# Seven block products in place of eight for a third of the feed-forward entry tiles of a two-layer encoder step, on one core

## The chip, the core and the metric

One core of a Trainium2 chip runs the whole program. The metric is the time of one execution on the device in microseconds (us), the median of several runs. The engines work side by side and meet only at semaphores: PE (TensorE, matmuls), DVE (VectorE), ACT (ScalarE), POOL (GpSimd) and SP (SyncE, which here issues most transfers). PEld is the weight load of a matmul.

## The reference, cut to what matters

Two request groups, 512 prompt tokens and 64 sample tokens, go through two layers with shared weights. Each layer is a feed-forward block (half step), a mixer (two kinds of attention, a spatial gate, and a merge of the three branches under gates) and a second feed-forward block. Shift, scale and gate of every normalization come from a vector c per group through a large matrix `w_ada`. In float32:

```
mp = silu(c) @ w_ada[l] + b_ada[l]                 # 9 modulation vectors of 1024 per layer
pre_mod(h, g, shift, scale) = rmsnorm(h, g) * (1 + scale) + shift
g, u = split(x @ w1)                               # x: 576 x 1024, w1: 1024 x 5504
swiglu(x) = (silu(g) * u) @ w2                     # 2752 -> 1024
h += 1/2 * gate * rmsnorm(swiglu(pre_mod(h)))      # feed-forward block, twice a layer
m = sig(gA)*(oA@W_a) + sig(gB)*(oB@W_b) + sig(gC)*(oC@W_c);  h += gate2 * rmsnorm(m @ W_out)
```

## The kernel before

Activations lie transposed: 128 features on the partitions, 576 tokens along them, in two halves of 288 (`columns(b)`). Every float32 product is three matmuls of rounded parts: weights and activations are each split in a high part (fp32r) and a low rest, and `w_hi*x_hi + w_hi*x_lo + w_lo*x_hi` is summed in PSUM. So one 128x128 weight block against 576 tokens is 6 matmuls (3 products, 2 halves), and one tile of 128 output features of the feed-forward entry (1024 inputs, 8 blocks) is 48.

**Weights** come in chunks of 128x1024 float32 (8 blocks, 512 KB) through a ring of 5 slots (`SLOTS`). SP issues the transfer for chunk c when PE is done with chunk c-5. ACT then writes `w_hi` (`split_hi`, L1296), DVE writes `w_lo = w_raw - w_hi` (`split_lo`, L1715; it lies where the raw chunk lies), and PE may start. The order of these steps among the other work of ACT and DVE is written out by hand.

**Feed-forward entry** (`f1a`, `f1b`, function `ffn_up`): 22 pairs i of a g tile and a u tile (43 chunks; pair 21 is a half-filled tail). In each pair PE makes g into PSUM pair 0 (banks 0 and 1) and u into PSUM pair 1 (banks 2 and 3). DVE takes each out of PSUM times `r2`, the reciprocal root mean square per token (`take`, L1792), since x is normalized only behind the product; the share of the shift comes from two more columns of the matmul (290 in place of 288). ACT does silu, DVE the product g*u, and both split it in `hid_hi` and `hid_lo`. PE may use a PSUM pair again when it has been taken (`acc_free`).

**Feed-forward exit** (`f2a`, `f2b`): 8 output tiles of 126 matmuls and a tail. **Gate stage** (`merge`, phase `gate`): for each of 8 tiles m, PE makes three gate tiles of 48 matmuls (br 0, 1, 2 into PSUM pairs 0, 1, 0) and then three branch products A, B, C of 12, 24 and 12 matmuls into pairs 1, 0, 1. A needs the release of gate tile br 1, B that of br 2 (the `sig` instruction, L2343, and the small one behind it), C that of A (`msum`, L2350).

**Modulation units**: what `w_ada` needs is cut in units of 128 outputs x 512 inputs, 256 in all. POOL issues the 256 KB transfer of a unit into one of two buffers (`ada_w`) when DVE has finished the unit two before it. DVE then does two multiply-and-sum instructions per unit (L1729), one for each group. Tables in the kernel (`ADA_STAGES`, `f1_units`, `f2_units`, `gate_units`) say how many units stand at each place of DVE's order: up to 3 in a pair of an entry, 2 at a step of the exits of layer 0, and 1 or 2 ahead of `sig` of br 1 and br 2 in the gate stage of layer 0. POOL otherwise only issues transfers.

Of the kernel before, what the change touches and what calls it, by code (L numbers as in the profile page):

```python
# [70 lines left out]
F1_CHUNKS = 2 * KF - 1  # L71
# [15 lines left out]
ADA_STAGES = [((0, "f1a"), (2, 4, 3)), ((0, "f2a"), (5, 7)), ((0, "gate"), (6,)), ((0, "f1b"), (8, 10, 9)),  # L87
              ((0, "f2b"), (11, 13)), ((1, "f1a"), (12, 14, 15)), ((1, "f2a"), (16,)), ((1, "gate"), ()),
              ((1, "f1b"), (17,)), ((1, "f2b"), ())]
AFTER_PAIRS = ((0, "gate"), (1, "f1b"))  # L90
# [33 lines left out]
def f1_units(l, ab, i):  # L124

    return 0 if i in (2, 11, KF - 2) else 1 if (l, ab) == (1, "b") else 3


def f2_units(l, ab):

    half = {(0, "a"): 8, (0, "b"): 8, (1, "a"): 4, (1, "b"): 0}[l, ab]
    return iter([2] * half + [0] + [2] * half + [0] * KF)


def gate_units(m):

    return {1: (1, 1), 2: (1, 2), 3: (1, 2), 4: (0, 0), 5: (1, 1), 6: (1, 2), 7: (1, 2)}.get(m, (0, 0))
# [16 lines left out]
def chunk(l, ph, i):  # L154
    return l * CHUNK_N + CHUNK_AT[ph][0] + i

# [215 lines left out]
def build_program(nc, ins, outs):  # L372
# [64 lines left out]

    rms = sb("rms", [P, 3, TOK], at=big + 2 * TOK * 4)
# [122 lines left out]
    hid_ready = S("hid_ready", 2 * KF)  # L561
# [29 lines left out]
    sil_ready = S("sil_ready", 2 * KF)  # L591
    g_scaled = S("g_scaled", 4)
# [79 lines left out]
    def _(sp):  # L672
# [38 lines left out]

        def exchange_tail(l, f):
# [6 lines left out]
        for l in range(DEPTH):  # L719
            for i in range(F1_CHUNKS):  # L720
                load(l, "f1a", i, ins["f1"], 2 * l * F1_CHUNKS + i)
                if l == 0 and i == 1:
                    first_ada(*FIRST_PARTS[1])
                if l == 0 and i == 2:
                    first_ada(*FIRST_PARTS[2])
                    first_ada(*FIRST_PARTS[3])
            for name, out in (("cache_a_k", "roll_k"), ("cache_a_v", "roll_v")):
# [15 lines left out]
            for i in range(F1_CHUNKS):  # L743
                load(l, "f1b", i, ins["f1"], (2 * l + 1) * F1_CHUNKS + i)
# [12 lines left out]
    def _(pe):  # L757
# [32 lines left out]
        def whole_chunk(l, ph, i, p, group, hi, lo, cols, gate=None):  # L790
# [8 lines left out]
            r.then_inc(chunk_done.sem, 1)  # L799

# [117 lines left out]
        def ffn(l, ab, n):  # L918
# [361 lines left out]
    def _(act):  # L1280
# [4 lines left out]
        def split_hi():  # L1285
# [5 lines left out]
            act.wait_ge(raw_full[c % SLOTS].sem, raw_full[c % SLOTS].done(0, c // SLOTS))  # L1291
# [5 lines left out]

        def chunk_over(l, ph, i):
            act.wait_ge(chunk_done.sem, chunk_done.done(0, chunk(l, ph, i)))

        def ffn_up(l, ab):
            ph, at = "f1" + ab, (0 if ab == "a" else KF + KD)
            mine = 0 if ab == "a" else KF
# [10 lines left out]
            for i in range(KF - 1):  # L1314
                if i == 1 and not l and ab == "a":
                    split_hi()
                if i < 2:
                    act.wait_ge(g_scaled.sem, g_scaled.done(l, (ab == "b") * 2 + i))
                else:
                    split_hi()  # L1320
                    act.wait_ge(acc_free[0].sem, acc_free[0].done(l, GROUP_AT[ph][0] + i - 1))
# [6 lines left out]
                if i > 1:  # L1328
                    split_hi()
            split_hi()  # L1330
# [3 lines left out]
            act.wait_ge(hid_ready.sem, hid_ready.done(l, mine + KF - 1))  # L1334
            copy(hid_hi[:, KF - 1, :], tail_hid[:, :]).then_inc(prod_hi.sem, 1)

# [379 lines left out]

# [963 lines left out]
```

## Time and profile before

| | us |
|---|---|
| median of 3 runs | 2680.75 (2680.7 to 2681.24) |
| the profiled execution | 2681.71 |
| its span, first to last instruction | 2679.8 |
| PE busy | 2645.8 (99%) |
| DVE busy | 1636.2 (61%) |
| ACT busy | 963.1 (36%) |
| POOL busy | 200.0 (7%), all but four tiny instructions the issue of transfers |

The page lists the busy time of each engine, then the chain of work that ended last, then groups of instructions with their mean duration. PE is busy all the time, and its clock was granted in full. So what matters is how many matmuls there are, and whether anything makes PE wait.

### The profile page before, as it was taken

Reading aid. Unit: us, or ns where it says so; the run is one execution under the profiler, and the core shown is the slowest. Engines: PE = TensorE matmul, PEld = TensorE weight load, DVE = VectorE, ACT = ScalarE, POOL = GpSimd, SP = SyncE. Lnnn points to the kernel's source line nnn. Section 1 sums busy time; section 2 is a strip of 40 time slices with the busy share of each in tenths; the row PEclk is TensorE's granted clock in tenths of the full one; section 3 lists DMA queues with packets and bytes.
Section 4 is the critical chain, followed back from the end, with each engine's and each line's share of the span. In section 5 each row is a group of like instructions: output and inputs, shape, how many; then the busy total and the mean of one; then the engine's idle time right before and its main releaser. Section 6 shows DMA issues by size and latency. Waiting matters only on the chain.

```text
span 2679.8 us, 49072 instructions
## 1 busy us (share of the span) xinstructions
PE 2645.8 (99%) x20698; PEld 2563.3 (96%) x20698; DVE 1636.2 (61%) x3542; ACT 963.1 (36%) x1792; POOL 200.0 (7%) x371
## 2 busy tenths in 40 slices
PE   7999999999999999999999999999999999999997
PEld 6999999888999999999999999998889999999997
DVE  4677666765555577776577776276655445555523
ACT  4232324444422442232252223255452336322321
POOL 0111010110000001111101111001100000000000
PEclk9999999999999999999999999999999999999998
DMA  6444453343333224445424444234332222333321
GB/s 261 126 146 141 157 177 113 124 130 109 95 111 111 87 95 154 136 144 168 131 89 152 139 159 161 88 98 141 119 105 80 87 83 76 99 109 105 95 82 65
DMA packets 92987, 324.79 MB, mean 121 GB/s; under 512 B 13980, under 2 KB 17628, under 8 KB 92064
## 3 DMA queue, kind: packets, MB, share of 16 engines
q1 hardware_dynamic: 62512, 221.72, 26.3%
q0 software_dynamic: 30256, 99.93, 11.2%
q8 instruction: 164, 2.69, 0.4%
q14 instruction: 55, 0.45, 0.1%
HBM read 310.70 MB, written 11.55 MB: 120 GB/s over the span
## 4 chain that ended last, share of the span: by engine, by line
PE 97%; DVE 1%; DMA 0%; issue 0%; ACT 0%; DVEq 0%; SPq 0%; ACTq 0%
PE ps L769 90%; PE ps L1131 2%; PE ps L1179 1%; PE ps L1155 1%; PE ps L778 1%; DMA ada_first<-in_ada_first 0%; PE ps L1148 0%; PE ps L823 0%; DVE prob L2242 0%; PE ps L909 0%; PE ps L1192 0%; DVE next L1792 0%; PE ps L807 0%; PE ps L832 0%; PE ps L1055 0%
## 5 line engine op out<-in xcount | busy, mean ns | idle before, releaser
L769 PE MATMUL ps<-x_hi,w_hi 128*128 128x288 f32 (+1 forms) x4224 | 938.9, 298 | 2.4 <-DVE x_lo L1883 1.5
L769 PE MATMUL ps<-x_lo,w_hi 128*128 128x288 f32 (+1 forms) x4224 | 922.5, 294 | 0.0
L769 PE MATMUL ps<-x_hi,w_lo 128*128 128x288 f32 (+1 forms) x4224 | 922.4, 294 | 0.0
L769 PEld LDWEIGHTS ps<-x_hi,w_hi 128*128 128x128 f32 x4224 | 682.6, 188 | 14.2 <-issue 8.0
L769 PEld LDWEIGHTS ps<-x_hi,w_lo 128*128 128x128 f32 x4224 | 685.7, 188 | 0.0
L769 PEld LDWEIGHTS ps<-x_lo,w_hi 128*128 128x128 f32 x4224 | 685.3, 188 | 0.3
L1715 DVE TENSOR_TENSOR w_lo<-w_raw,w_hi 128x1024 fp32r<-128x1024 f32 x384 | 468.1, 1222 | 160.1 <-ACT w_hi L1296 158.1
L1296 ACT CAST w_hi<-w_raw 128x1024 fp32r<-128x1024 f32 x384 | 391.9, 1048 | 72.4 <-DMA w_raw<-in_f 71.6
L769 PE MATMUL ps<-hid_hi,w_hi 128*128 128x288 f32 x1344 | 301.1, 295 | 0.0
L769 PE MATMUL ps<-hid_lo,w_hi 128*128 128x288 f32 x1344 | 299.3, 293 | 0.0
L769 PE MATMUL ps<-hid_hi,w_lo 128*128 128x288 f32 x1344 | 299.0, 294 | 0.0
L1729 DVE CUSTOM_DVE_ANT_0 ps<-ada_w,c_half,ada_all 128x512 f32<-128x512 f32 x256 | 193.6, 756 | 108.8 <-DMA ada_w<-in_ada 108.6
L2432 POOL DMA_DIRECT2D ada_w<-in_ada x256 | 138.1, 540 | 1626.6 <-DVE ada_all L1729 1622.1
L769 PEld LDWEIGHTS ps<-hid_hi,w_hi 128*128 128x128 f32 x1344 | 219.8, 188 | 0.2
L769 PEld LDWEIGHTS ps<-hid_lo,w_hi 128*128 128x128 f32 x1344 | 219.4, 188 | 0.2
L769 PEld LDWEIGHTS ps<-hid_hi,w_lo 128*128 128x128 f32 x1344 | 217.2, 187 | 0.0
L1327 ACT CAST hid_hi<-hid 128x576 fp32r<-128x576 f32 x84 | 56.6, 674 | 446.7 <-DVE hid L1765 446.7
L1729 DVE CUSTOM_DVE_ANT_0 ada_w<-ada_w,c_half,ada_all 128x512 f32<-128x512 f32 x256 | 191.5, 748 | 0.0
L1323 ACT ACTIVATE sil<-sil,z 128x512 f32<-128x512 f32 (+1 forms) x168 | 80.9, 529 | 248.6 <-DVE z L1793 248.4
L1792 DVE TENSOR_TENSOR hid<-ps,r 128x576 f32<-128x576 f32 x80 | 60.6, 758 | 146.9 <-PE ps L769 146.9
L1808 DVE TENSOR_TENSOR acc_y<-acc_y,sq 128x576 f32<-128x576 f32 (+1 forms) x51 | 33.0, 646 | 179.5 <-ACT sq L1367 153.7
L1367 ACT ACTIVATE sq<-ps 128x576 f32<-128x576 f32 x38 | 24.9, 654 | 296.1 <-PE ps L778 263.2
(243 smaller groups left out, 2440.4 us busy)
## 6 DMA issues: line engine op xcount, KB each, us to landing
w_raw<-in_f SPq DMA_DIRECT2D x260, 512.0 KB, 3.7
ada_w<-in_ada POOLq DMA_DIRECT2D x256, 256.0 KB, 4.0
w_raw<-in_gate SPq DMA_DIRECT2D x64, 512.0 KB, 3.6
w_raw<-in_tri SPq DMA_DIRECT2D x40, 512.0 KB, 3.7
ada_first<-in_ada_first SPq DMA_DIRECT2D x4, 2048.0 KB, 21.0
w_raw<-in_wout SPq DMA_DIRECT2D x16, 512.0 KB, 3.6
c_half<-c_scratch POOLq DMA_DIRECT2D x11, 512.0 KB, 5.6
decay_p<-f_prompt POOLq DMA_DIRECT2D x8, 512.0 KB, 4.5
```

Source lines behind the costliest of these rows:

```text
L769: r = mm(ps[:, 2 * out + b, 0:width], w, xx[:, cols(b)], start=first and n == 0, stop=last and n == 2)
L778: r = mm(ps[:, 2 * out + b, 0:HALF], w[:, s, t * P:(t + 1) * P], hid_hi[:, k, columns(b)], start=False, stop=w is w_lo)
L1131: r = mm(out, q_st[rows, i * P:i * P + m], k, start=True, stop=True)
L1155: r = turn_in(out, prob[0:m, place(u), b * P:b * P + w], const[0:m, IDENT, 0:m])
L1296: copy(w_hi[:, c % SLOTS, :], w_in[:, c % SLOTS, :]).then_inc(hi_ready.sem, 1)
L1323: r = A(sil[:, i, part], sil[:, i, part], ACT.Silu, bias=c_col[:, 2 * (i % 2), g:g + 1])
L1327: copy(hid_hi[:, i, :], hid[:, i, :]).then_inc(prod_hi.sem, 1)
L1715: V.tensor_tensor(w_lo[:, s, :], w_in[:, s, :], w_hi[:, s, :], ALU.subtract).then_inc(lo_ready.sem, 1)
L1729: r = V.tensor_tensor_reduce(out, ada_w[:, u % 2, :], c_half[:, g, :], 1.0, so_far, ALU.mult, ALU.add, so_far)
L1792: V.tensor_tensor(two(dst), pair[p], two(r2[:, :]), ALU.mult)
L1808: V.tensor_tensor(total, total, more, ALU.add).then_inc(y_added.sem, 1)
L2432: nc.gpsimd.dma_start(dst, src).then_inc(signal.sem, 16)
```

## The change

**Seven products.** In pairs 6 to 12 (`JOIN0` to `JOIN1`) of each of the four entries, g and u tile of a pair are made together. The inputs are cut in two halves of 512 features, the tokens in two halves of 288, the weights in four block columns (g or u, lower or upper inputs): a 2x2 by 2x2 block product, done with 7 half products of 12 matmuls (4 blocks, 3 parts, 288 tokens) in place of 8. It needs sums of weight blocks (4 additions of 128x512 a pair, done by POOL in place in the raw slots, `sum_of_w`), sums of blocks of x (`t_sums`, once an entry), and 7 additions of a 128x288 product out of PSUM (`join_parts`, DVE). A pair is now four chunks (three of 1024 columns, one of 512) whose high and low parts ACT and DVE make behind the sums.

**x normalized ahead.** The block sums need plain x. So DVE multiplies h by `r2` (`h_times_r2`), ACT adds scale and shift (`full_of_h`), both split the result again while pair 3 runs (`high_of_full`, `low_of_full`; pair 3 and pair 4 go through the inputs g and u in step), and from pair 4 on g and u need no `r2` and no shift columns: ACT reads g from PSUM in its silu, DVE multiplies u out of PSUM.

**Modulation units moved.** Pairs 3 to 12 have none any more. The tables put 5, 5, 6, 0, 4, 4, 4, 4 of them in pairs 13 to 20 (three of the four entries), 32 in place of 16 in the exit `f2a` of layer 1, 32 in place of 16 in the gate stage of layer 0 and 16 in place of 0 in that of layer 1. There are 256 as before. In the diff, `load_joined` is in the program of SP, `joined_pair` in that of PE, `joined_stage` in that of DVE and `sum_of_w` in that of POOL.

```diff
-def f1_units(l, ab, i):
-    return 0 if i in (2, 11, KF - 2) else 1 if (l, ab) == (1, "b") else 3
+def f1_units(l, ab, i):
+    if (l, ab) == (1, "b"):
+        return 2 if i >= JOIN1 else 0
+    return {13: 5, 14: 5, 15: 6, 17: 4, 18: 4, 19: 4, 20: 4}.get(i, 0)
...
-    half = {(0, "a"): 8, (0, "b"): 8, (1, "a"): 4, (1, "b"): 0}[l, ab]
+    half = {(0, "a"): 8, (0, "b"): 8, (1, "a"): 8, (1, "b"): 0}[l, ab]
...
-def gate_units(m):
-    return {1: (1, 1), 2: (1, 2), 3: (1, 2), 4: (0, 0), 5: (1, 1), 6: (1, 2), 7: (1, 2)}.get(m, (0, 0))
+def gate_units(l, m):
+    if l == 0:
+        return {1: (2, 3), 2: (2, 3), 3: (3, 3), 5: (2, 3), 6: (2, 3), 7: (3, 3)}.get(m, (0, 0))
+    return {1: (1, 1), 2: (1, 2), 3: (1, 2), 5: (1, 1), 6: (1, 2), 7: (1, 2)}.get(m, (0, 0))
...
+        def load_joined(l, ab, i):
...
+                sp.wait_ge(chunk_done.sem, chunk_done.done(0, c + v - SLOTS))
+                spare_read(l, ab, c + v)
...
+        def joined_pair(l, ab, i):
...
+            part(0, 0, 0, *x_block(0, 0)).then_inc(half_done.sem, 1)
+            part(1, 0, 1, *t_block(2)).then_inc(chunk_done.sem, 1)
+            part(2, 1, 0, *t_block(1)).then_inc(half_done.sem, 1)
+            part(3, 1, 1, *t_block(3)).then_inc(chunk_done.sem, 1)
+            part(4, 2, 0, *t_block(0)).then_inc(half_done.sem, 1)
+            part(5, 2, 1, *x_block(half_k, 0)).then_inc(chunk_done.sem, 1)
+            part(6, 3, 0, *x_block(half_k, 1)).then_inc(chunk_done.sem, 1)
...
+        def joined_stage(l, ab, i):
+            more = i + 1 < JOIN1
+            if i > JOIN0:
+                low_of_joined(l, ab, i, 2)
+                low_of_hid(l, ab, i - 1)
+            join_parts(l, ab, i, 0)
+            join_parts(l, ab, i, 1)
+            if i > JOIN0:
+                low_of_joined(l, ab, i, 3)
+            join_parts(l, ab, i, 2)
+            join_parts(l, ab, i, 3)
+            join_parts(l, ab, i, 4)
+            if more:
+                low_of_joined(l, ab, i + 1, 0)
...
+            join_parts(l, ab, i, 5)
+            join_parts(l, ab, i, 6)
+            if more:
+                low_of_joined(l, ab, i + 1, 1)
...
+            product_of_joined(l, ab, i)
...
+        def sum_of_w(l, ab, i, order):
...
+            if order == 0:
+                pool.wait_ge(raw_full[g].sem, raw_landed(c))
...
+            elif order == 1:
+                pool.wait_ge(w_sum.sem, w_sum.done(l, at))
+                pool.wait_ge(raw_full[u].sem, raw_landed(c + 1))
...
+            elif order == 2:
+                pool.wait_ge(w_sum.sem, w_sum.done(l, at + 1))
+                pool.wait_ge(chunk_done.sem, chunk_done.done(0, c + 3 - SLOTS))
...
+            else:
+                pool.wait_ge(raw_full[more].sem, raw_landed(c + 2))
...
+            nc.gpsimd.tensor_tensor(*operands, ALU.add).then_inc(w_sum.sem, 1)
```

The order of DVE in the gate stage of layer 0, tile m=1, from the low part of a weight chunk through the units to `sig` of br 2, before (an ISA row over ps or ada_w is one of a unit's two instructions, the short rows read its sum):

```order
L1715 TENSOR_TENSOR w_lo<-w_raw,w_hi 128x1024 [waits hi_ready]
L1729 ISA ps,ada_all<-ada_w,c_half,ada_all 128x512 [waits ada_full1]
L1729 ISA ada_all 128x1
L1729 ISA ada_w,ada_all<-ada_w,c_half,ada_all 128x512
L1729 ISA ada_all 128x1
L2343 TENSOR_TENSOR sig<-ps,r_71 128x576 [waits chunk_done]
L2344 TENSOR_SCALAR z<-ps,b_gate 128x2
```

And DVE in the same place of the changed kernel, from the second of the three units that now stand behind the low part:

```order
L2112 ISA ps,ada_all<-ada_w,c_half,ada_all 128x512 [waits ada_full1]
L2112 ISA ada_all 128x1
L2112 ISA ada_w,ada_all<-ada_w,c_half,ada_all 128x512
L2112 ISA ada_all 128x1
L2112 ISA ps,ada_all<-ada_w,c_half,ada_all 128x512 [waits ada_full0]
L2112 ISA ada_all 128x1
L2112 ISA ada_w,ada_all<-ada_w,c_half,ada_all 128x512
L2112 ISA ada_all 128x1
L2772 TENSOR_TENSOR sig<-ps,r_71 128x576 [waits chunk_done]
L2773 TENSOR_SCALAR z<-ps,b_gate 128x2
```

Ahead of `sig` of br 2, which releases PSUM pair 0 for branch product B, stand three units where one stood here (two at m=2 and 3), on two buffers.

The order of DVE from the middle of one joined pair into the next in the changed kernel, where `ps` rows of 128x288 take products out of PSUM:

```order
L2057 TENSOR_TENSOR sil<-sil,ps 128x288 [waits half_done]
L2057 TENSOR_TENSOR hid<-hid,ps 128x288 [waits joined]
L2002 TENSOR_TENSOR w_lo<-w_raw,w_hi 128x1024 [waits hi_ready,w_sum]
L2057 TENSOR_TENSOR sil<-sil,ps 128x288 [waits chunk_done]
L2057 TENSOR_TENSOR sil<-sil,ps 128x288 [waits joined,chunk_done]
L2002 TENSOR_TENSOR w_lo<-w_raw,w_hi 128x1024 [waits hi_ready,w_sum]
L2064 SCALAR_TENSOR_TENSOR hid<-hid,sil 128x576 [waits joined,sil_half]
L2002 TENSOR_TENSOR w_lo<-w_raw,w_hi 128x1024 [waits hi_ready,w_sum]
L2070 TENSOR_TENSOR hid_lo<-hid,hid_hi 128x576 [waits prod_hi]
```

Before, a pair's low parts followed two PSUM reads of 128x576; now the low part that the next pair starts with stands behind the fifth of seven reads of 128x288, and it also waits for POOL's sums (`w_sum`).

## Rows read from the trace of the kernel before

**Rows 1.** The page: busy us (share of the span) and instructions of each engine.

```profile
PE 2645.8 (99%) x20698; PEld 2563.3 (96%) x20698; DVE 1636.2 (61%) x3542; ACT 963.1 (36%) x1792; POOL 200.0 (7%) x371
```

**Rows 2.** The chain that ended last: start us, us, what ran.

```profile
355.21 16.58 PE ps L769 x126
...
423.66 8.29 PE ps L769 x63
...
689.01 233.08 PE ps L769 x1767
...
955.26 267.83 PE ps L769 x2034
...
2005.73 233.51 PE ps L769 x1767
...
2557.89 16.59 PE ps L769 x126
```

**Rows 3.** Stages: us, busy us (instructions) by engine, clock, DMA share, GB/s.

```profile
690.00:922.00 232.00, 232.00 (x1763) 232.00 (x1762) 129.00 (x210) 75.66 (x122) 9.34 (x17) 1.00 0.33 102
...
955.00:1223.00 268.00, 268.00 (x2037) 267.95 (x2036) 193.35 (x400) 81.40 (x113) 27.67 (x51) 1.00 0.42 136
```

**Rows 4.** DVE by form: xcount, busy us, mean ns, idle before and its releaser.

```profile
L1715 DVE TENSOR_TENSOR w_lo<-w_raw,w_hi 128x1024 fp32r<-128x1024 f32 x384 | 468.1, 1222 | 160.1 <-ACT w_hi L1296 158.1
L1729 DVE CUSTOM_DVE_ANT_0 ps<-ada_w,c_half,ada_all 128x512 f32<-128x512 f32 x256 | 193.6, 756 | 108.8 <-DMA ada_w<-in_ada 108.6
...
L1770 DVE TENSOR_TENSOR hid_lo<-hid,hid_hi 128x576 fp32r<-128x576 f32 x84 | 63.8, 759 | 62.2 <-ACT hid_hi L1327 62.2
...
L1792 DVE TENSOR_TENSOR hid<-ps,r 128x576 f32<-128x576 f32 x80 | 60.6, 758 | 146.9 <-PE ps L769 146.9
...
L1849 DVE SCALAR_TENSOR_TENSOR rms<-ps,rms 128x288 f32<-128x288 f32 x12 | 5.5, 455 | 0.2
```

**Rows 5.** DVE in time, gate stage, m=5: start us, us, instruction [idle before].

```profile
765.17 0.76 DVE L2343 TENSOR_TENSOR sig<-ps,r 128x576 f32<-128x576 f32 x1 [0.90 <-PE ps L769]
765.84 0.21 DVE L2344 TENSOR_SCALAR z<-ps,b_gate 128x2 f32<-128x2 f32 x1
768.02 1.23 DVE L1715 TENSOR_TENSOR w_lo<-w_raw,w_hi 128x1024 fp32r<-128x1024 f32 x1 [1.97 <-ACT w_hi L1296]
769.16 0.75 DVE L1729 CUSTOM_DVE_ANT_0 ps<-ada_w,c_half,ada_all 128x512 f32<-128x512 f32 x1
...
771.86 0.75 DVE L2343 TENSOR_TENSOR sig<-ps,r 128x576 f32<-128x576 f32 x1
772.52 0.21 DVE L2344 TENSOR_SCALAR z<-ps,b_gate 128x2 f32<-128x2 f32 x1
773.18 0.76 DVE L2350 TENSOR_TENSOR msum<-sig,ps 128x576 f32<-128x576 f32 x1 [0.45 <-PE ps L769]
```

**Rows 6.** DVE in time, exit of layer 0, two groups of two units.

```profile
345.74 0.76 DVE L1729 CUSTOM_DVE_ANT_0 ps<-ada_w,c_half,ada_all 128x512 f32<-128x512 f32 x1 [1.19 <-DMA ada_w<-in_ada]
...
347.09 0.76 DVE L1729 CUSTOM_DVE_ANT_0 ps<-ada_w,c_half,ada_all 128x512 f32<-128x512 f32 x1
...
352.18 0.76 DVE L1729 CUSTOM_DVE_ANT_0 ps<-ada_w,c_half,ada_all 128x512 f32<-128x512 f32 x1 [2.52 <-DMA ada_w<-in_ada]
```

**Rows 7.** POOL in time, the same stretch: issues of the units' transfers.

```profile
341.41 0.54 POOL L2432 DMA_DIRECT2D ada_w<-in_ada  x1 [4.28 <-DVE ada_all L1729]
...
347.47 0.54 POOL L2432 DMA_DIRECT2D ada_w<-in_ada  x1 [3.89 <-DVE ada_all L1729]
```

**Rows 8.** The page: transfers, KB each, median us from issue to landing.

```profile
w_raw<-in_f SPq DMA_DIRECT2D x260, 512.0 KB, 3.7
ada_w<-in_ada POOLq DMA_DIRECT2D x256, 256.0 KB, 4.0
```

**Rows 9.** DVE in time, a pair of an entry: two instructions beside POOL's issues.

```profile
179.30 1.22 DVE L1715 TENSOR_TENSOR w_lo<-w_raw,w_hi 128x1024 fp32r<-128x1024 f32 x1
...
187.37 1.23 DVE L1715 TENSOR_TENSOR w_lo<-w_raw,w_hi 128x1024 fp32r<-128x1024 f32 x1 [0.19 <-ACT w_hi L1296]
```

**Rows 10.** POOL in time, the same pair.

```profile
179.65 1.09 POOL L2432 DMA_DIRECT2D ada_w<-in_ada  x2
```

More of the change, by code:

```diff
@@ L799, in whole_chunk, with chunk_pair @@
             r.then_inc(chunk_done.sem, 1)
+        def chunk_pair(l, ph, i, pairs, cols, ab):
+            c = chunk(l, ph, 2 * i)
+            chunk_ready(c)
+            chunk_ready(c + 1)
+            for k in range(KD):
+                n = (ab == "b") * KD + k
+                if i == NORMED:
+                    pe.wait_ge(x_full_ready.sem, x_full_ready.done(l, n))
+                for s in (0, 1):
+                    r = split_tile(pairs[s], c + s, k, x_hi[:, k, :], x_lo[:, k, :], cols, k == 0, k == KD - 1)
+                    if k == KD - 1:
+                        r.then_inc(chunk_done.sem, 1)
+                if i < NORMED and k < KD - 1:
+                    r.then_inc(x_read.sem, 1)
@@ L1313, in ffn_up @@
                 split_hi()
-            for i in range(KF - 1):
+            for i in range(NORMED):
                 if i == 1 and not l and ab == "a":
@@ L1327, in ffn_up @@
                 copy(hid_hi[:, i, :], hid[:, i, :]).then_inc(prod_hi.sem, 1)
-                if i > 1:
+                if i == 1:
                     split_hi()
+                    for k in range(KD):
+                        full_of_h(l, ab, k)
+                        if k == 3:
+                            split_hi()
+            for i in range(NORMED, KF - 1):
+                if JOIN0 <= i < JOIN1:
+                    joined_parts(l, ab, i)
+                    continue
+                if i == JOIN1:
+                    high_of_hid(l, ab, i - 1)
+                if i == JOIN0 - 1:
+                    high_of_joined(l, ab, JOIN0, 0)
+                    high_of_joined(l, ab, JOIN0, 1)
+                else:
+                    split_hi()
+                if i == NORMED:
+                    for order, t in enumerate((2, 1, 3, 0)):
+                        high_of_t(l, ab, t, order)
+                act.wait_ge(chunk_done.sem, chunk_done.done(0, chunk(l, ph, f1_chunk(i))))
+                A(two(sil[:, i, :]), pair[0], ACT.Silu).then_inc(acc_free[0].sem, 1)
+                if i == JOIN0 - 1:
+                    high_of_joined(l, ab, JOIN0, 2)
+                    high_of_joined(l, ab, JOIN0, 3)
+                    continue
+                if i > NORMED:
+                    split_hi()
+                act.wait_ge(acc_free[1].sem, acc_free[1].done(l, GROUP_AT[ph][1] + f1_group(1, i)))
+                copy(hid_hi[:, i, :], hid[:, i, :]).then_inc(prod_hi.sem, 1)
             split_hi()
@@ L1768, in ffn_up @@
                 r.then_inc(hid_ready.sem, 1)
+                if i == 1:
+                    for k in range(2, KD, 2):
+                        h_times_r2(k)
                 dve.wait_ge(prod_hi.sem, prod_hi.done(l, at + i))
```

394 lines of the change are left out of this document (350 added, 44 removed).

## The prediction, made before the changed kernel ran

> **What bounds the kernel now.** I read three views, in this order. The page's busy times: PE 99%, DVE 61%, POOL 7% [rows 1]. The chain that ended last: it is PE nearly throughout, in pieces of hundreds of matmuls without a break; an entry is 2034 matmuls in 267.83 us, so one matmul costs 0.1317 us. A run of 63 in which each follows the last into the same PSUM bank takes 8.29 us, 0.1316 each [rows 2]. So the pace does not hang on alternating banks, which half products of 12 don't do, nor on 290 or 288 columns, so that dropping the shift columns is worth nothing. The stages: in an entry DVE is busy 193 of 268 us, in the gate stage of layer 0 129 of 232, and that stage's chain (233.08) is no longer than layer 1's (233.51), which has no modulation units [rows 2, 3]. So nothing but the number of matmuls sets the end, and a change gains 0.1317 us for each matmul it drops as long as DVE, ACT, POOL and the transfers stay out of PE's way.
>
> **Part 1, seven products.** 84 matmuls a pair in place of 96: 12 x 0.1317 = 1.58 us. 7 pairs x 4 entries = 28 pairs: **-44.2 us**, if PE runs through. A pair is then 84 x 0.1317 = 11.06 us.
>
> DVE in such a pair: three low parts of 1024 columns (1.22) and one of 512 (0.69, on the line through the rows of 576 and 1024), seven additions out of PSUM (0.455), the product and the low part of `hid` (0.76 each) [rows 4]. 3.66 + 0.69 + 3.19 + 1.52 = 9.06 of 11.06 us. It fits, with 2 us to spare. The place without slack is the low part that the next pair starts with. It stands behind the additions of product 4; product 4 ends two products (24 matmuls, 3.16 us) before the pair does; 0.2 until DVE sees it, two additions 0.91, the low part 1.22: 0.8 us are left. That makes PE wait for nothing, by these rows.
>
> POOL's sums: the trace has no addition on POOL. The chain through them is: sum 2 may start behind product 5 (1.58 us before the pair ends), then sum 3, then a low part of 1.22 that is needed 24 matmuls (3.16 us) into the next pair. 1.58 + 3.16 - 1.22 - 0.2 = 3.3 us for two sums, so up to 1.65 us each they cost nothing. Lower bound 0.69 (DVE's own pace): 0. Upper bound 2.44, twice DVE's row for 1024 columns: 2 x (2.44 - 1.65) = 1.6 us a pair, all of the gain. The nearest rows are the 0.69 to 1.22 of DVE [rows 4], so I take 0.
> The Trainium skill (GPSIMD Engine Reference, section 3) has an addition of 2048 float32 columns at 4497 ns on GpSimd against 2293 ns on VectorE; by that pace a sum of 512 is, as an estimate of mine, about 1.2 us, and the term stays at 0.
>
> **Part 2, x ahead.** In pairs 2 to 5 DVE gets 3 x 1.36 (`h_times_r2`, 1152 columns on the line through the rows of 576 and 1024), 8 x 0.76 (low parts of x), 8 x 1.36 (block sums of x and their low parts), and loses all units and half of the PSUM takes: some 42 us of the 50.6 that four pairs last. What a pair needs stands half a pair or more ahead. I take 0; the bounds are 0 (no matmul is dropped here, so nothing can be gained) and 2 us an entry, one late low part.
>
> **Part 3, the units.** This is what I think decides. In the gate stage [rows 5] `sig` of br 2 starts at 771.86, at once behind the second of two units that began at 769.16, so a unit takes 1.35 us. The release of PSUM pair 0 is at about 772.7; PE has then nearly finished branch A (its `msum` starts at 773.18) and goes on to B into that pair. So the slack is 0.3 us, and the two units just fit. Now three stand there, and there are two buffers. In an exit one sees how fast a buffer comes back [rows 6, 7]: the unit that began at 345.74 ended at 347.09, POOL issued at 347.47, and DVE, waiting for it, began at 352.18: 5.09 us from a unit's end to the next in the same buffer. (The page's 4.0 [rows 8] is the median of all landings; here another transfer was under way, as it will be.) So:
> - (2, 3), at m=1, 2, 5, 6. Two units ahead of br 1 delay its `sig` by 0.4 (765.17 to 765.6) and the following low part to 768.4. Units 3 and 4 run to 770.9 and 772.25. Unit 5 needs unit 3's buffer: 770.9 + 5.09 = 776.0, ends 777.35. `sig` and its small follower take 0.9: 778.2. B could have begun at 773.0: **5.2 us** of waiting PE, four times, 20.8.
> - (3, 3), at m=3, 7. The third unit ahead of br 1 waits for its buffer to 769.3, so `sig` of br 1 comes at 770.65, just in time for A. The next low part ends at 774.6, units at 775.95, 777.3, and the last at 781.05 + 1.35 = 782.4; release 783.3: **10.3 us**, twice, 20.6.
> Gate stage of layer 0: **+41.4 us**. The pattern of layer 1 is the one that layer 0 had before [rows 5]: 0. Exit `f2a` of layer 1 gets layer 0's pattern, which holds up nothing: its tiles of 126 matmuls take 16.58 us each, as in the last exit, which has no units [rows 2]: 0.
>
> Entries, pairs 13 to 20. Two buffers give one unit per (1.35 + 5.09) / 2 = 3.2 us. Count from the end of u of pair 13, with the units in groups of 2 | 3, 2 | 3, 3 | 3 around the products, and about 1.2 and 0.7 for low parts between: the third unit of a group waits 3.7. Product 14 is done at 17.6 (PE needs it at 19.0), the next eight units put product 15 at 37.0, and PE needs it at 5 x 6.32 = 31.6: **5.4 us**. Pair 16 has no unit and DVE catches up; 4 units a pair (12.9 of 12.64 us) hold to the end. Three entries have this table: **+16.2 us**. If the buffer came back in 4.0 + 0.4 us, both terms would be 36 and 9.
>
> **Part 4, POOL and DVE side by side.** Does a POOL instruction that reads and writes SBUF hold up DVE? A low part beside two of POOL's issues takes 1.22 us, without any 1.23 [rows 9, 10], but an issue is no addition. Bounds: 0, and a full exclusion of each sum from the low parts. Then sum 1 puts 1.0 us ahead of the third low part, the additions move on, DVE comes to the critical low part after sum 2 has begun (product 5 is done by then) and waits 1.2 more: 1.0 + 1.2 - 0.8, minus 0.2 that the additions of products 0 and 1 had spare, is 1.2 us a pair, 34 us in all. I take 0.3 us a pair, since only one of four sums falls on the place without slack and the rows lean to none: **+8.4 us**.
> The Trainium skill (SBUF — State Buffer, section "Who interferes with whom") says that a DVE instruction with two SBUF inputs and a GpSimd instruction that reads SBUF exclude each other for their whole length. No row here shows it; by that rule the sum would take the upper end, and it is rival B.
>
> **Sum.** -44.2 + 41.4 + 16.2 + 8.4 = +21.8 us. The profiled execution is 2681.71 (span 2679.8), 0.96 over the median, so span 2701.6, that execution 2703.5, median 2680.75 + 21.8 = **2702.5**.
>
> **Rivals.**
> A, the forecast: the units' buffers make PE wait, the joined pairs run nearly free. 2702; with 36 and 9 for the terms of part 3 and 0 for part 4 it is 2681.5, with 12 more in part 4 2715. Chance 0.42.
> B, exclusion in full: joined pairs of 12.3 us give 10 us back instead of 44. 2680.75 + 57.6 - 10.2 = 2728. For: DVE has only 0.8 us at the critical place. Against: no row. Chance 0.25. It decides from 0.8 us of delay of that low part.
> C, faster: the buffers are no limit. If every transfer were there in time, three units cost 4.05 where 2.7 fitted: `sig` of br 2 released at 774.5, PE waits 1.5 us six times, 9 us, and none in the entries. 2680.75 - 44.2 + 9 = 2646. For: the median landing of 4.0 [rows 8] is shorter than the 4.7 I used. Against: DVE waits for its units at both groups of the exit, 1.19 and 2.52 us [rows 6], although only two stand in each. Chance 0.2.
> D, the seven products don't pay at all: sums over 1.65 us or late low parts stretch a pair to 12.64. 2680.75 + 57.6 = 2738 or more. Chance 0.08. The rest, 0.05, is what I haven't seen.
>
> **How the numbers follow.** The likeliest is A: 2702. For 8 in 10, the range takes most of A, B and the slow half of C: **2658 to 2734**. A measurement of this kernel tells 0.2% (5.4 us) from no change. Faster by more: most of C, 0.2. Within: between C and A, with short landings, 0.12. Slower: 0.68.
>
> **What would show it.** In the profile after: PE matmuls 20698 - 336 = 20362. The chain of a joined pair 11.06 us (A) or some 12.3 (B). In the gate stage of layer 0 a wait of PE for the `sig` instruction of br 2, six times, 5 to 10 us, the stage near 274 us and layer 1's still 233. In three entries one wait of PE in pair 16 for the product, about 5 us. DVE's wait for `ada_w` well over the 108.8 us of before [rows 4]. POOL additions near 1 us. If the gate stage stays at 233, part 3 is wrong and the kernel is faster; if DVE's low parts are longer than 1.22 in pairs 6 to 12, part 4 is.

## The result and the profile after

| | before | after |
|---|---|---|
| median of the runs, us | 2680.72 (2680.33 to 2681.24) | 2727.7 (2725.95 to 2729.09) |
| ratio to before | | 1.0175, interval 1.0157 to 1.0192 |
| profiled execution; its span, us | 2681.71; 2679.8 | 2725.95; 2724.0 |
| granted clock, mean over the span | 0.997 | 0.985 |

The changed kernel is 47 us slower; 2702 was forecast, 21.8 slower. The sign is right and the time lies in the range, but the loss is more than twice the forecast. The first page lines of after, which answer to [rows 1] and [rows 8] (busy us, share of the span, instructions; the clock in 40 slices; transfers with KB each and median us to landing):

```profile
PE 2630.2 (97%) x20362; PEld 2543.7 (93%) x20362; DVE 1731.3 (64%) x3522; ACT 1069.6 (39%) x1920; POOL 362.4 (13%) x484
...
PEclk9999999999989999999999999999999999999998
...
ada_w<-in_ada POOLq DMA_DIRECT2D x256, 256.0 KB, 3.4
```

PE has the 20362 matmuls that were forecast, 336 fewer, and yet is busy only 15.6 us less, in a span 44.2 us longer. So there are two losses: 60 us more in which PE stands, and some 29 us in which what it does takes longer (the 336 dropped matmuls were 44.2 us of work, and its busy time fell by only 15.6).

The chain that ended last says where (start us, us, what ran). The joined pairs of the first entry, the gate stage of layer 0 with the piece behind it, and the gate stage of layer 1; [rows 2] has the gate stages before:

```profile
114.82 77.98 PE ps L934 x588
...
724.29 13.39 PE ps L875 x84
756.82 14.17 PE ps L875 x84
792.19 38.82 PE ps L875 x276
849.66 13.83 PE ps L875 x84
882.70 12.74 PE ps L875 x84
916.67 49.53 PE ps L875 x363
966.69 9.87 PE ps L875 x75
...
2048.60 233.15 PE ps L875 x1767
```

588 matmuls of seven joined pairs take 77.98 us, 11.14 a pair: PE runs through. The gate stage of layer 0, one piece of 1767 matmuls before, has come apart: six pieces of it show here, each behind a wait, and between them the chain runs through DVE; layer 1's is one piece still. By the starts of the same piece in both chains the account is (us, after less before; what has gathered since the start of the program):

| at the start of | before | after | gathered | this stage |
|---|---|---|---|---|
| exit, layer 0, first | 320.98 | 317.79 | -3.2 | entry -3.2 |
| behind the gate stage, layer 0 | 922.57 | 966.69 | +44.1 | gate stage +47.3 |
| exit, layer 0, second | 1223.62 | 1266.97 | +43.3 | entry -0.8 |
| exit, layer 1, first | 1637.54 | 1680.29 | +42.7 | entry -0.6 |
| behind the gate stage, layer 1 | 2239.73 | 2282.24 | +42.5 | -0.2 |
| exit, layer 1, second | 2540.78 | 2582.88 | +42.1 | entry -0.4 |

Behind the last matmul some 2 us more follow (2.5 in the kernel with the tables alone, below, which has eight products; what makes them stays open). So the gate stage loses 47.3 us, and the entries, each with 84 matmuls less (-11.05 us), give 0.4 to 3.2. PE's waits of after (line that waits, releaser: us in total, times, longest):

```profile
PE ps L875 <- DVE z L2773: 33.4, 6, 7.0
PE ps L875 <- ACT sil L1579: 13.6, 4, 4.7
...
PE ps L875 <- DVE w_lo L1992: 11.0, 5, 3.2
...
PE ps L875 <- DVE hid L2187: 0.6, 2, 0.4
```

L2773 is the small instruction behind `sig` of br 2. (A wait of 11.1 at the program's start, left out, was there before.) L1579 is the silu of the plain g tiles, L1992 a low part outside the joined pairs: both belong to the entries, and neither is in the forecast. L2187 is the product of g and u, for which 5.4 us in pair 16 of three entries were forecast.

**The gate stage.** The chain there at m=2, from the end of the first unit behind the low part to PE's start at 756.82 (start us, us, what); it answers to [rows 5]:

```profile
749.19 0.61 DVE ada_w L2112
...
750.10 4.41 DMA ada_w<-in_ada
...
755.97 0.67 DVE sig L2772
756.64 0.14 DVE z L2773
```

The unit ends at 749.8, POOL issues, and the transfer lands at 754.5: 4.7 us from a unit's end to the next in its buffer. Then the third unit, `sig`, and PE may go on. PE waited 4.92 us. It then needed 14.17 us for 84 matmuls that take 11.06 at full pace. The stage in stretches around the wait at m=1 (stretch, us, then busy us and count of PE, PEld, DVE, ACT, POOL, granted clock, DMA share, GB/s):

```profile
709.00:719.00 10.00, 10.00 (x78) 10.00 (x77) 7.13 (x19) 1.90 (x3) 1.61 (x3) 1.00 0.41 113
...
724.30:729.00 4.70, 4.70 (x20) 4.70 (x21) 1.82 (x2) 1.86 (x3) 0.00 (x0) 0.52 0.17 56
729.00:738.00 9.00, 9.00 (x70) 9.00 (x69) 5.31 (x7) 1.63 (x2) 0.00 (x0) 1.00 0.23 61
```

Behind the wait the granted clock is 0.52, the lower level of 1.2 GHz for nearly all of 4.7 us, and PE is busy throughout with 20 matmuls where 36 would fit. Then it is 2.4 GHz again. The pieces behind the six waits take 54.1 us for four times 84 matmuls, 38.8 for 276 and 49.5 for 363; at 0.1317 each they would take 44.2, 36.3 and 47.8: 14.1 us lost to the clock. 33.4 + 14.1 = 47.5, the 47.3 of the table.

**The entries.** PE's timeline, the waits in the second entry (start us, us, instruction [idle before, releaser]), the chain that leads to each (as above), and the stretches behind them:

```profile
1019.95 0.82 PE L875 MATMUL ps<-x_hi,w_hi 128*128 128x288 f32 x2 [3.17 <-DVE w_lo L1992]
```

```profile
1013.47 3.81 DVE x_full L2210 x3
...
1018.67 1.14 DVE w_lo L1992
...
1019.95 15.53 PE ps L875 x96
...
1046.60 1.37 DVE t_raw L2015
1047.99 2.21 ACT t_hi L1493 x2
1050.20 0.56 ACT sil L1579
...
1050.89 12.88 PE ps L875 x96
```

```profile
1019.95:1027.00 7.05, 7.05 (x33) 7.05 (x34) 1.59 (x5) 6.04 (x13) 0.00 (x0) 0.59 0.00 0
1050.90:1058.00 7.10, 7.10 (x54) 7.10 (x55) 6.36 (x6) 3.09 (x4) 0.72 (x2) 1.00 0.05 20
```

At the start of pair 3, g and u go through the inputs in step, so PE needs the low parts of both chunks (6 and 7) at once. That of chunk 7 stands in DVE's order behind the last three `h_times_r2`, 3.81 us together in the chain: PE waits 3.17 us, and needs 15.53 us for 96 matmuls instead of 12.64. At the start of pair 5 PE needs PSUM pair 0, which ACT releases with its silu of g tile 4; in ACT's order it stands behind the high parts of the block sums (`t_hi`), and these behind DVE's sums (`t_raw`): 2.79 us more. g and u of pair 4 end together, so there is no u tile in between to hide it. 3.17 + 2.89 + 2.79 + 0.24 = 9.1 us of the 11.05 that the entry gains. Seven joined pairs lose another 0.8 (78.25 us for the 77.43 of 588 matmuls at full pace).

**DVE and POOL.** Groups by form (count, busy us, mean ns, idle before), for [rows 4]:

```profile
L2002 DVE TENSOR_TENSOR w_lo<-w_raw,w_hi 128x1024 fp32r<-128x1024 f32 x84 | 102.2, 1220 | 34.8 <-POOL w_raw L2895 34.8
L2070 DVE TENSOR_TENSOR hid_lo<-hid,hid_hi 128x576 fp32r<-128x576 f32 x68 | 67.6, 995 | 7.9 <-ACT hid_hi L1509 4.9 <-ACT hid_hi L1587 3.0
...
L2895 POOL TENSOR_TENSOR w_raw<-w_raw 128x512 f32<-128x512 f32 x112 | 162.3, 1460 | 599.3 <-DMA w_raw<-in_f 516.5 <-issue 51.5 <-PE ps L875 29.7
```

A sum takes 1.46 us on average. The low parts of `hid`, 0.759 before, take 0.995, those of 512 columns 0.850; those of 1024, 1.22, are as they were.

### The profile page after: what moved, and what is told of

The parts are those of the page before. It is cut to its first block, busy times and chain, and to the rows that moved or that the text cites. A ratio compares the mean times of both kernels' runs of the same rounds, so it can differ in the third digit from the quotient of the medians.

```text
span 2724.0 us, 49060 instructions
## 1 busy us (share of the span) xinstructions
PE 2630.2 (97%) x20362; PEld 2543.7 (93%) x20362; DVE 1731.3 (64%) x3522; ACT 1069.6 (39%) x1920; POOL 362.4 (13%) x484
## 4 chain that ended last, share of the span: by engine, by line
PE 83%; DVE 8%; DMA 3%; ACT 3%; issue 1%; DVEq 1%; POOL 0%; SPq 0%; ACTq 0%
PE ps L875 64%; PE ps L934 11%; DMA ada_w<-in_ada 3%; PE ps L1314 2%; DVE w_lo L1992 1%; PE ps L1362 1%; PE ps L1338 1%; DVE ada_w L2112 1%; DVE ps L2112 1%; ACT w_hi L1479 1%; PE ps L884 1%; ACT x_full L1600 1%; DVE hid L2156 0%; DMA ada_first<-in_ada_first 0%; DVE sig L2772 0%
## 5 line engine op out<-in xcount | busy, mean ns | idle before, releaser
L875 PE MATMUL ps<-x_hi,w_hi 128*128 128x288 f32 (+1 forms) x3328 | 754.5, 301 | 27.2 <-ACT sil L1579 13.6
L875 PE MATMUL ps<-x_lo,w_hi 128*128 128x288 f32 (+1 forms) x3328 | 736.8, 296 | 0.0
L875 PE MATMUL ps<-x_hi,w_lo 128*128 128x288 f32 (+1 forms) x3328 | 736.1, 295 | 0.0
L875 PEld LDWEIGHTS ps<-x_hi,w_hi 128*128 128x128 f32 x3328 | 542.1, 189 | 41.2 <-issue 33.8
L875 PEld LDWEIGHTS ps<-x_lo,w_hi 128*128 128x128 f32 x3328 | 545.3, 189 | 0.3
L875 PEld LDWEIGHTS ps<-x_hi,w_lo 128*128 128x128 f32 x3328 | 545.1, 189 | 0.0
L1992 DVE TENSOR_TENSOR w_lo<-w_raw,w_hi 128x1024 fp32r<-128x1024 f32 x328 | 399.4, 1222 | 149.5 <-ACT w_hi L1479 146.7
L1479 ACT CAST w_hi<-w_raw 128x1024 fp32r<-128x1024 f32 x328 | 340.2, 1048 | 75.7 <-DMA w_raw<-in_f 74.9
L2895 POOL TENSOR_TENSOR w_raw<-w_raw 128x512 f32<-128x512 f32 x112 | 162.3, 1460 | 599.3 <-DMA w_raw<-in_f 516.5
L2002 DVE TENSOR_TENSOR w_lo<-w_raw,w_hi 128x1024 fp32r<-128x1024 f32 x112 | 126.0, 1127 | 34.9 <-POOL w_raw L2895 34.8
L934 PE MATMUL ps<-t_hi,w_hi 128*128 128x288 f32 x448 | 132.9, 297 | 0.1
```

Source lines behind the costliest of these rows:

```text
L875: r = mm(ps[:, 2 * out + b, 0:width], w, xx[:, cols(b)], start=first and n == 0, stop=last and n == 2)
L934: r = mm(ps[:, bank, 0:HALF], w, moved, start=k == 0 and m == 0, stop=k == half_k - 1 and m == 2)
L1479: copy(w_hi[:, c % SLOTS, :], w_in[:, c % SLOTS, :]).then_inc(hi_ready.sem, 1)
L1992: V.tensor_tensor(w_lo[:, s, :], w_in[:, s, :], w_hi[:, s, :], ALU.subtract).then_inc(lo_ready.sem, 1)
L2002: V.tensor_tensor(w_lo[:, s, 0:n], w_in[:, s, 0:n], w_hi[:, s, 0:n], ALU.subtract).then_inc(lo_ready.sem, 1)
L2895: nc.gpsimd.tensor_tensor(*operands, ALU.add).then_inc(w_sum.sem, 1)
```

## The experiments

Each ran beside the kernel before, on the same chip; ratios are to that.

### The unit tables alone

The kernel before, with eight products, and the tables of the units as in the changed kernel for the gate stages and the exits; its entries have two units a pair where three stood. The two lines that matter:

```diff
-    return 0 if i in (2, 11, KF - 2) else 1 if (l, ab) == (1, "b") else 3
+    return 0 if i in (2, 11, KF - 2) else 1 if (l, ab) == (1, "b") else 2
...
+        return {1: (2, 3), 2: (2, 3), 3: (3, 3), 5: (2, 3), 6: (2, 3), 7: (3, 3)}.get(m, (0, 0))
```

> The kernel before, all eight products, with the changed kernel's unit tables for the gate stages and exits (entries with two units a pair where three stood). Theory: the gate stage of layer 0 alone costs what it costs in the changed kernel, six waits of 5 to 7 us and the clock's falls, 47 us: 2728. Rival (the waits come from something that the joined products leave behind): no change, 2681.

Measured: 2728.74 us (2727.69 to 2731.04), ratio 1.0179 (1.0164 to 1.0194). Its waits at `sig`:

```profile
PE ps L771 <- DVE z L2346: 32.8, 6, 6.7
```

The tables alone cost 48 us, 46 of it in this stage by the starts in the chain. So the loss of the changed kernel is that of its gate stage (47.3 of 44.2 us), and all else in it adds up to a gain of 3.1.

### Even groups in the gate stage

The same 32 units, at most two in a row, the rest behind the low part of the merge at the tile's end:

```diff
-        return {1: (2, 3), 2: (2, 3), 3: (3, 3), 5: (2, 3), 6: (2, 3), 7: (3, 3)}.get(m, (0, 0))
+        return {1: (2, 2, 1), 2: (2, 2, 1), 3: (2, 2, 1), 4: (1, 0, 0), 5: (2, 2, 1), 6: (2, 2, 1), 7: (2, 2, 2)}.get(m, (0, 0, 0))
...
+                ada(l, "gate", gate_units(l, m)[2])
```

> The changed kernel; in the gate stage of layer 0 its 32 units stand two ahead of br 1, two ahead of br 2 and one behind the tile's last step, so that no group has three. Theory (third unit waits for its buffer, PE for sig of br 2, and the clock falls behind each wait): the six waits of PE and the clock's falls go, the stage returns from 280 to 233 us, the kernel from 2727.7 to about 2681. Rival (it is the amount of DVE's work in that stage, 32 units however they stand): waits of PE remain, the stage stays above 255, the kernel above 2700.

Measured: 2685.59 us (2682.38 to 2690.05), ratio 1.0018 (1.0009 to 1.0028): 42.1 less than the changed kernel. One wait of the stage is left, the pieces behind it are near full pace, and the waits of the entries are still there (at the low part 10.5 us):

```profile
PE ps L875 <- ACT sil L1579: 16.4, 4, 4.8
...
PE ps L875 <- DVE z L2773: 0.7, 1, 0.7
...
720.53 11.35 PE ps L875 x84
```

So it is not the number of units in the stage but the third in a row. The 2681 expected is missed by some 4 us: the stage is still 2.9 us longer than before (the last wait of 0.7 and 0.3 us in each of six pieces), and the entries give 2.5 us less than in the changed kernel.

### A third unit's work without its buffer

The even groups, and two more multiply-and-sum instructions ahead of `sig` of br 2, which read the buffer that is there: the work of a third unit without the wait for a transfer. The edit also puts a `drain` (DVE lets what it has begun come to its end) ahead of three of the four instructions of that unit.

```diff
-                for g in (0, 1):
+                for g in (0, 0, 0, 1) if more and u % 2 else (0, 1):
```

> The kernel of the even groups in the gate stage, with the two multiply-and-sum instructions more behind one of the two units ahead of br 2, so that DVE does the work of three units on two transfers; this makes the modulations wrong. Theory (of the 5 us that a third unit costs, 1.35 are its work and 3.4 the wait for its buffer): PE waits some 1.5 us seven times, the clock falls little, the stage is 10 to 15 us longer than with even groups. Rival (DVE's work alone makes the waits of 5 to 7 us): the stage is over 30 us longer.

Measured, one run: 2706.04 us, 20.5 more than with the even groups, between the 10 to 15 expected and the rival's 30. PE waits six times at `sig`, 14.6 us in all. Timeline of PE at the first two waits, the stretches behind these and behind the fourth, and two of the added instructions on DVE ahead of the second wait:

```profile
723.21 0.85 PE L875 MATMUL ps<-o_hi,w_hi 128*128 128x288 f32 x2 [3.63 <-DVE z L2775]
753.64 0.54 PE L875 MATMUL ps<-o_hi,w_hi 128*128 128x288 f32 x2 [2.19 <-DVE z L2775]
...
723.20:730.00 6.80, 6.79 (x31) 6.79 (x32) 2.42 (x3) 1.88 (x3) 0.00 (x0) 0.56 0.12 39
753.60:760.00 6.40, 6.36 (x46) 6.36 (x47) 4.23 (x6) 1.90 (x3) 0.03 (x1) 1.00 0.24 78
834.80:841.00 6.20, 6.20 (x35) 6.20 (x36) 2.87 (x4) 1.87 (x3) 0.00 (x0) 0.72 0.11 44
...
748.15 0.76 DVE L2114 CUSTOM_DVE_ANT_0 ps<-ada_w,c_half,ada_all 128x512 f32<-128x512 f32 x1
749.08 0.76 DVE L2114 CUSTOM_DVE_ANT_0 ps<-ada_w,c_half,ada_all 128x512 f32<-128x512 f32 x1
```

The first wait has 1.35 us of DVE's wait for a buffer in it; the other five are 2.18 to 2.19 us, where 1.5 were expected. But these five hold the drains: behind a drain the next instruction comes 0.93 us after the one before it (748.15, 749.08, and again 750.01) where it comes after 0.67 without one, some 0.7 us in all. Without them about 1.5 us are left for the work, as expected. With its buffer the wait is 4.4 to 5.0 us at (2, 3), so about a third of it is work and the rest the buffer. Of the 20.5 us the waits are 13.9 and the longer pieces behind them some 6: behind 3.63 us the clock was 0.56 for 6.8 us, and behind the five waits of 2.2 us it was 1.00 three times and fell twice (0.72 over 6.2 us behind the fourth, the same over 6.1 us behind the sixth).

### Three joined pairs less

`JOIN1` is 10 in place of 13: pairs 10 to 12 of each entry have eight products again, and 144 matmuls come back.

```diff
-JOIN0, JOIN1 = 6, 13
+JOIN0, JOIN1 = 6, 10
```

> The changed kernel with 4 joined pairs (6 to 9) in each entry in place of 7; pairs 10 to 12 by eight products, without units. Theory (joined pairs run at PE's pace): 12 pairs more by 12 matmuls each, 144 x 0.1317 = 19 us slower than the changed kernel, 2747. Rival (joined pairs are held up by POOL's sums): less than 10 us slower.

Measured: 2746.63 us (2745.04 to 2747.42), ratio 1.0243 (1.0226 to 1.026), 18.9 more. 12 pairs at 1.58 us are 18.96. A joined pair pays what its matmuls say; next to nothing of the entries' loss lies in them.

### Sums filled, sums doubled

POOL writes a constant in place of each sum (so the sums, and the outputs with them, are left out), and, in another kernel, makes each sum twice, with a `drain` between (the edit of the first):

```diff
-            nc.gpsimd.tensor_tensor(*operands, ALU.add).then_inc(w_sum.sem, 1)
+            nc.gpsimd.memset(operands[0], 1.0).then_inc(w_sum.sem, 1)
```

> The changed kernel with POOL filling its blocks with ones in place of adding weight blocks, which leaves the sums out: POOL writes as much but reads nothing. Theory (a DVE instruction with two SBUF inputs and a POOL addition hold each other up): DVE's low parts of hid return from 995 to about 758 ns and those of 512 columns from 850 to about 690; the kernel's time stays within 3 us. Rival (these are long for another reason, such as their semaphore): they stay long.

> The changed kernel with each of POOL's additions done twice, which makes other sums. Theory (sum 2 and sum 3 have 3.3 us between product 5 and the low part that PE needs): two sums of 2.9 us exceed it by 2.6 us, and with the holding up of DVE a joined pair takes 13.5 to 15 us in place of 11.1, the kernel is 70 to 110 us slower. Rival (the sums have far more room than that): under 20 us.

Measured, one run each: 2726.12 us with the fills and 2821.96 with the sums twice. A group by form of the first, a wait of PE in the second:

```profile
L2070 DVE TENSOR_TENSOR hid_lo<-hid,hid_hi 128x576 fp32r<-128x576 f32 x68 | 51.1, 752 | 7.9 <-ACT hid_hi L1509 4.9 <-ACT hid_hi L1587 3.0
```

```profile
PE ps L934 <- DVE w_lo L2002: 70.7, 52, 3.0
```

Without additions the low parts of `hid` are at 0.752 us and those of 512 columns at 0.684: it was the additions that held DVE up. It costs no time: 2726.12 is within the runs of the changed kernel. Doubled, the sums cost 94 us, 3.4 a pair: there the chain through them is late. So there is a limit, and one sum of 1.46 us is on the near side of it; that it lies at the computed 1.65 us isn't shown, since nothing between one sum and two was run.

### The late steps of the entries

Only the silu of g tile 4, ahead of the last two high parts of the block sums:

```diff
+                    for order, t in enumerate((2, 1)):
                         high_of_t(l, ab, t, order)
                 act.wait_ge(chunk_done.sem, chunk_done.done(0, chunk(l, ph, f1_chunk(i))))
                 A(two(sil[:, i, :]), pair[0], ACT.Silu).then_inc(acc_free[0].sem, 1)
+                if i == NORMED:
+                    for order, t in ((2, 3), (3, 0)):
+                        high_of_t(l, ab, t, order)
```

> The changed kernel with only one step in another order: ACT's silu of g tile 4 ahead of the last two of the four high parts of the block sums. Theory (it is one of two places in each entry): the wait for silu goes from 2.8 to 4.8 us to about 1, the one of 3.2 us for the low part of chunk 7 stays, 2 to 5 us an entry, 2708 to 2720. Rival (DVE's block sums are late as well and silu does not matter): under 1 us an entry.

Measured: 2716.86 us (2715.24 to 2717.16), ratio 1.0132 (1.0117 to 1.0147), 10.8 less than the changed kernel. That is inside the 2708 to 2720 expected. The silu waits go from 13.6 to 6.4 us; the rest of the 10.8 is mostly the clock, which fell behind the longer waits.

The same, and the low part of chunk 7 behind the second `h_times_r2` in place of the fourth:

```diff
-                    for k in range(2, KD, 2):
+                    h_times_r2(2)
+                    split_lo()
+                    for k in range(4, KD, 2):
                         h_times_r2(k)
```

> The changed kernel with two steps of each entry in another order: ACT's silu of g tile 4 ahead of the last two of the four high parts of the block sums of x, and DVE's low part of chunk 7 ahead of two of the four multiplications of h by r2. Theory (pairs 3 and 5 start late by 3.2 and 2.8 to 4.8 us, and the clock falls behind the wait, together 9 to 10 us an entry): each entry shortens by 6 to 9 us, the kernel to 2692 to 2704. Rival (ACT and DVE simply have too much work in pairs 1 to 5, a late step is replaced by the next): under 3 us an entry, 2716 or more.

Measured: 2713.8 us (2712.45 to 2718.01), ratio 1.0125 (1.011 to 1.014), 13.9 less than the changed kernel, 3.5 an entry where 6 to 9 were expected. Moving the low part of chunk 7 added only 3 us, and PE's waits for low parts outside the joined pairs stay at 9.7 us in all (10.5 without the move, 11.0 in the changed kernel): in their sum one late step was replaced by the next, as the rival had it. With the even groups as well:

> Both edits together. Theory: the effects add, 2645 to 2657, faster than the kernel before (2680.7) by 24 to 36 us. The limit is 2680.7 - 44 = 2637. Rival: one of the rivals above, 2670 or more.

Measured: 2668.54 us (2667.5 to 2670.69), ratio 0.9955 (0.994 to 0.9969): 59.2 less than the changed kernel, where the two edits alone give 42.1 and 13.9, 56.0 together. They add up, so gate stage and entries are two separate losses. It is slower than the 2645 to 2657 expected, and PE's timeline in the second entry shows why:

```profile
983.53 0.50 PE L875 MATMUL ps<-x_hi,w_hi 128*128 128x288 f32 x2 [2.85 <-DVE w_lo L1995]
```

The wait at the start of pair 3 is gone and has come back one pair on: the low part of chunk 9, behind the low parts of x, is now the late one. Behind this wait the clock fell too (0.76 over 7 us).

### All late steps taken forward

Even groups; the silu ahead of all high parts of the block sums; the low part of chunk 7 as above, that of chunk 8 ahead of the product of pair 2 and that of chunk 9 right behind it, with ACT's high part of chunk 9 behind the silu of pair 2.

```diff
                     take(hid[:, i, :], 1, 1).then_inc(acc_free[1].sem, 1)
+                    split_lo()
                 else:
                     for k in range(KD):
                         low_of_full(l, ab, k)
-                        if k in (2, 5):
+                        if k == 5:
                             split_lo()
...
+                if i == 2:
+                    split_lo()
                 dve.wait_ge(prod_hi.sem, prod_hi.done(l, at + i))
```

> Even groups in the gate stage and a further order of the entries: ACT does silu of g tile 4 ahead of all high parts of block sums; DVE makes the low part of chunk 7 behind the second multiplication of h by r2, that of chunk 8 ahead of the product of pair 2, and that of chunk 9 right behind it, ACT the high part of chunk 9 behind its silu of tile 2. Theory (the start of pair 4 still waits 2.9 us for the low part of chunk 9, and pair 5 1 to 3 us for silu of tile 4): both waits fall under 1 us and the clock stays up, 3 to 6 us an entry less than with the first order (2668.5), so 2645 to 2657. Rival (ACT's 16 instructions on x are the bound, in whatever order): 2664 or more.

Measured: **2653.57 us** (2652.84 to 2654.62), ratio 0.9897 (0.9881 to 0.9914), the fastest of all: 27.6 less than the kernel before and 74.1 less than the changed one. The waits of its joined pairs, and pieces of the chain in the second entry:

```profile
PE ps L934 <- DVE w_lo L2004: 5.1, 3, 1.7
...
948.15 42.69 PE ps L875 x324
...
1005.67 78.22 PE ps L934 x588
```

By the dropped matmuls alone it would be some 44 us under before, 16.6 more. These are found: what lies between the first exit and the end of the gate stage of layer 0 is 3.2 us longer than before (six branch pieces, each 0.3 over full pace, and 1.1 of waits at `sig` are of it), the last three entries are shorter by 7.4 to 8.1 instead of 11.05, 10.2 in all, the first by 10.3, and the 2 us behind the last matmul are there again. In the second entry 1.7 of the 3.5 us are a wait of the first joined pair for its low part, behind two sums and the low parts of the block sums.

## Why the prediction was right or wrong, point by point

**What bounds the kernel**: right. Where nothing makes PE wait, the matmul takes 0.1317 us, 0.1326 to 0.1333 in joined pairs, and dropping matmuls pays nearly in full (28 pairs of 11.14 to 11.19 us each against the 11.06 forecast, 2.8 us in all). **Part 1**, -44.2, holds but for 0.1 us a pair. The sums at 1.46 us, under the 1.65 up to which they were to be free, cost nothing that the run with fills would have given back; doubled, they do.

**Part 3, gate stage**: the mechanism was right, in place, number and cause. Six waits at `sig` of br 2; two of 7.0 us where groups of (3, 3) stand and four of 4.4 to 5.0 where groups of (2, 3) do; forecast were 10.3 and 5.2. A unit's buffer came back in 4.7 us at the place shown, 5.09 by [rows 6, 7], and at (3, 3), m=3, its transfers took only 3.1 and 3.0 us. So the waits were over-sized: 33.4 for 41.4 us. The stage still lost 47.3, since the sum had **no term for the clock**. This is the first step that failed: each wait was priced at its own length, and the matmuls behind it at the pace of PE without a break. The granted clock behind them was near half for some microseconds, which cost 14.1 us in this stage. That the total of the stage came out within 6 us of the forecast is two errors of opposite sign, and so luck.

**Part 3, entries**: +16.2 forecast, 0.6 us measured in all (the wait for `hid`). The buffer's return was mis-sized here: the unit stretch of the first entry, from the chain (start us, us, what),

```profile
214.90 2.67 DMA ada_w<-in_ada
224.50 4.35 DMA ada_w<-in_ada
```

has landings of 2.7 to 4.4 us where one row of an exit had given 4.7. The text's own "36 and 9" for short landings was nearer, and still too much. Where DVE waited for a buffer there, 3.1 to 4.8 us had gone by from the end of the unit before in it, 3.9 on average, and not 5.09. The product of pair 15, forecast 37.0 us behind the end of u of pair 13, was done at 31.5, just when PE needs it (31.6).

**Part 2**: taken as 0 with a bound of 2 us an entry, measured at 9 to 10 (in the first entry 7). This is the second failed step, and the larger, about 36 us over the four entries: they gave 5.0 us, where the matmuls dropped, less 2.8 for the joined pairs and 0.6 for the units' wait, would have given 40.8. The sentence was that "what a pair needs stands half a pair or more ahead"; it was never set against the order of the two engines, step by step, as the joined pairs were. Busy time fitted (42 of 50.6 us); two steps were late. Both follow from one thing in the diff, that g and u go in step: two weight chunks are needed at once where one was, and both PSUM pairs are released together at the end. That the late steps are the cause is shown by the silu and low-part experiments as far as they went, and by the last kernel, in which both waits are gone and three of the entries gain 7.4 to 8.1 us. That they are late because g and u go in step is read from the diff and the chain; no run took the step away.

**Part 4**: the mechanism is real and its price is 0, not 8.4. Additions lengthen two of DVE's forms, but neither is the low part on the critical place; that keeps its 1.22 us, and POOL's sum beside it is the one that waits.

**The rivals.** B named 2728 and the kernel took 2727.7, but not for B's reason: exclusion does happen, and joined pairs take 11.14 to 11.19 us, not 12.3. That the number fits is luck. C's price of 1.5 us for a third unit without its buffer was 2.2 in the run that tried it, of which some 0.7 were that run's drains. D falls with the three joined pairs taken out. In sum: -44.2 + 2.8 (joined pairs) + 47.3 (gate stage) + some 36 (pairs 1 to 5) + 0.6 (units) + 2 (behind the last matmul) = 44.5, for the profiled difference of 44.2; the medians lie 47.0 apart, since the profiled execution was the fastest of the four.

## What to carry to other kernels

A wait of TensorE of over 3.3 us cost here its length and some 1.5 to 3 us more in matmuls at the lower clock, and many waits of 2.2 to 3.2 us had such a price too: look for such a wait in the profile, read what the matmuls behind it take, and put that in the sum. When work is moved, walk each engine's order past the moved step for every stage that changes, those without any gain of their own too: the joined pairs were walked and were right, pairs 2 to 5 were judged by busy time and made the largest error. And check a table of helpers' work (here units on two buffers) by its longest group, not by its sum.

## What the runs showed of the hardware that was not expected

**TensorE's clock.** Behind waits of 3.17, 3.63, 4.92 and 5.02 us the granted clock was at or near its lower level of 1.2 GHz for some microseconds (0.52 over 4.7 us, 0.56 over 6.8, 0.59 over 7.05) and PE lost 2.3 to 3.1 us. Ahead of the one of 5.02 us PE had been busy without a break, at 1.00. The length of a wait alone doesn't say whether the clock falls. In the traces of the changed kernel and of six of the experiments (even groups, a third unit's work, silu alone, both late steps, these with the even groups, all late steps), by the granted clock of the 4 us behind each wait, and past the first 45 us of each, it was 1.00 behind all waits of 0.97 to 1.77 us and fell behind all 28 of 3.34 us and more; in between, waits of one length went both ways: of the five of 2.2 us it fell behind two, of fifteen of 2.58 to 2.94 us behind seven, of twelve of 3.17 to 3.19 us behind nine. Each trace is one execution, so whether the same wait goes the same way every time isn't shown.

**DVE and POOL.** Timelines of the changed kernel in a joined pair, DVE and then POOL:

```profile
140.19 1.22 DVE L2002 TENSOR_TENSOR w_lo<-w_raw,w_hi 128x1024 fp32r<-128x1024 f32 x1
141.32 1.85 DVE L2070 TENSOR_TENSOR hid_lo<-hid,hid_hi 128x576 fp32r<-128x576 f32 x1
143.09 0.44 DVE L2057 TENSOR_TENSOR sil<-sil,ps 128x288 f32<-128x288 f32 x1
```

```profile
140.77 1.78 POOL L2895 TENSOR_TENSOR w_raw<-w_raw 128x512 f32<-128x512 f32 x1 [2.43 <-DMA w_raw<-in_f]
143.09 1.30 POOL L2895 TENSOR_TENSOR w_raw<-w_raw 128x512 f32<-128x512 f32 x1 [0.54 <-DMA w_raw<-in_f]
```

The sum that begins at 140.77 beside a running low part takes 1.78 us instead of 1.30, as if it began when that ended (141.3 + 1.3 = 142.6); the low part of `hid` at 141.32 takes 1.85 us instead of 0.75, as if it began when the sum ended. The addition out of PSUM at 143.09, beside the next sum, takes its usual 0.44. By the Trainium skill (SBUF — State Buffer, section "Who interferes with whom") a VectorE instruction with two SBUF inputs and a GpSimd instruction that reads SBUF exclude each other, and one with at most one SBUF input, outside the modes that use both ports, does not; this trace agrees with both, and the run with fills, which only write, agrees as well (0.752 us). The estimate of 1.2 us for a sum, from the Trainium skill (GPSIMD Engine Reference, section 3), stands beside 1.30 where nothing is in the way and 1.46 on average.
